# Expert jobs with a limit of 96 rows instead of 128 in a two-layer decoder kernel

## The reference

```python
def moe_swiglu(x, w_router, w_gate, w_up, w_down):
    B, S, D = x.shape                       # 1, 256, 1024
    xt = x.reshape(B * S, D)
    logits = jnp.matmul(xt, w_router, preferred_element_type=jnp.float32)
    top_vals, top_idx = lax.top_k(logits, TOP_K)          # 2 of 8
    top_w = jax.nn.softmax(top_vals, axis=-1)
    gates = jnp.sum(jax.nn.one_hot(top_idx, N_EXPERTS, dtype=jnp.float32) * top_w[..., None], axis=1)
    out = jnp.zeros((B * S, D), jnp.float32)
    for e in range(N_EXPERTS):
        y = swiglu(xt, w_gate[e], w_up[e], w_down[e]).astype(jnp.float32)   # D_FF = 3584
        out = out + gates[:, e:e + 1] * y
    return out.astype(x.dtype).reshape(B, S, D)
```

## Time and profile before

| | us |
|---|---|
| median of 3 runs | 1458.99 (1458.88 to 1460.97) |
| the profiled execution | 1458.9 |
| of it: up to the first expert matmul | 494.9 |
| one job, from its row transposes to those of the next | 119.3 |
| TensorE busy | 1442.7 |
| DVE, ACT, POOL busy | 1142.1, 970.2, 110.0 |

### The profile page before, as it was taken

One profiled execution on the slowest core, in us unless ns is written; L12 is line 12 of the kernel. 1 busy time (PEld: TensorE's weight loads), 2 busy tenths in 40 slices (PEclk: granted clock), 3 DMA queues, 4 the chain that ended last, 5 costly groups with the idle time before them and its releaser, 6 DMA issues.

```text
span 1458.9 us, 19214 instructions
## 1 busy us (share of the span) xinstructions
PE 1442.7 (99%) x6982; PEld 1189.6 (82%) x6982; DVE 1142.1 (78%) x841; ACT 970.2 (66%) x820; POOL 110.0 (8%) x186
## 2 busy tenths in 40 slices
PE   9999999999999999999999999999999999999998
PEld 7857888888998888888888888888888888888886
DVE  5756445545555798989898899989898999888997
ACT  5445444334566677777787787787777778777775
POOL 3002000001000540010010010010001001000001
PEclk9999999999999999999999999999999999999999
DMA  8709555553643599999999999999999999999995
GB/s 263 273 1 331 196 179 173 197 192 115 217 145 116 183 382 384 362 394 383 364 383 394 363 371 397 369 362 399 383 353 388 388 369 376 392 371 364 383 380 189
DMA packets 177458, 445.88 MB, mean 306 GB/s; under 512 B 8770, under 2 KB 19074, under 8 KB 161284
## 3 DMA queue, kind: packets, MB, share of 16 engines
q1 hardware_dynamic: 173440, 431.56, 81.4%
q0 software_dynamic: 3968, 13.69, 2.7%
q10 hardware_dynamic: 4, 0.01, 0.0%
HBM read 437.33 MB, written 7.90 MB: 305 GB/s over the span
## 4 chain that ended last, share of the span: by engine, by line
PE 91%; DVE 3%; ACT 3%; issue 2%; DMA 0%; ACTq 0%; POOL 0%; DVEq 0%
PE psum L485 27%; PE psum L487 27%; PE psum L486 27%; PE psum L608 2%; PE psum L1070 2%; ACT w_hi L1252 2%; DVE w_lo L1670 1%; PE psum L444 1%; PE psum L467 1%; PE psum L797 0%; PE psum L788 0%; PE psum L474 0%; PE psum L721 0%; PE psum L1102 0%; PE psum L855 0%
## 5 line engine op out<-in xcount | busy, mean ns | idle before, releaser
L1670 DVE TENSOR_TENSOR w_lo<-raw,w_hi 128x2048 fp32r<-128x2048 f32 x378 | 861.9, 2292 | 180.2 <-ACT w_hi L1252 179.0
L1252 ACT ACTIVATE w_hi<-raw 128x2048 fp32r<-128x2048 f32 x378 | 724.6, 1919 | 270.4 <-PE psum L487 270.3
L485 PE MATMUL psum<-w_hi,x_hi 128*128 128x512 f32 (+2 forms) x1216 | 476.7, 392 | 2.9 <-DVE w_lo L1670 2.6
L487 PE MATMUL psum<-w_hi,x_lo 128*128 128x512 f32 (+2 forms) x1216 | 470.0, 386 | 0.0
L486 PE MATMUL psum<-w_lo,x_hi 128*128 128x512 f32 (+2 forms) x1216 | 469.3, 386 | 0.0
L485 PEld LDWEIGHTS psum<-w_hi,x_hi 128*128 128x128 f32 x1216 | 228.4, 188 | 50.2 <-DVE w_lo L1670 5.5
L487 PEld LDWEIGHTS psum<-w_hi,x_lo 128*128 128x128 f32 x1216 | 228.3, 188 | 46.1
L486 PEld LDWEIGHTS psum<-w_lo,x_hi 128*128 128x128 f32 x1216 | 228.7, 188 | 43.0
L485 PE MATMUL psum<-w_hi,h_hi 128*128 128x512 f32 x576 | 225.3, 391 | 0.0
L487 PE MATMUL psum<-w_hi,h_lo 128*128 128x512 f32 x576 | 224.2, 389 | 0.0
L486 PE MATMUL psum<-w_lo,h_hi 128*128 128x512 f32 x576 | 224.1, 389 | 0.0
(11 more groups left out here) (276 smaller groups left out, 971.8 us busy)
## 6 DMA issues: line engine op xcount, KB each, us to landing
raw<-in_l_w_gate SPq DMA_DIRECT2D x126, 1024.0 KB, 7.3
raw<-in_l_w_up SPq DMA_DIRECT2D x126, 1024.0 KB, 7.6
raw<-in_l_w_down SPq DMA_DIRECT2D x126, 1024.0 KB, 7.2
raw<-in_l_w_in SPq DMA_DIRECT2D x10, 1024.0 KB, 6.4
raw<-in_l_w_out SPq DMA_DIRECT2D x8, 1024.0 KB, 5.9
raw<-in_l_w_in SPq DMA_DIRECT2D x6, 768.0 KB, 14.2
raw<-in_l_w_mem_kv SPq DMA_DIRECT2D x4, 1024.0 KB, 5.9
ys<-xn SPq DMA_DIRECT2D x4, 512.0 KB, 8.5
```

The costliest lines, as they stand in the source:

```text
L485: pe.matmul(out, x[0], w[0], start=first, stop=False, skip_group_check=True)
L487: return pe.matmul(out, x[1], w[0], start=False, stop=last, skip_group_check=True)
L1252: act.activation(w_hi[:, m % CUT, :], raw[:, n % RAW, :], ACT.Copy).then_inc(hi_ok, 1)
L1670: dve.tensor_tensor(w_lo[:, m % CUT, :], raw[:, n % RAW, :], w_hi[:, m % CUT, :].bitcast(F32), ALU.subtract).then_inc(lo_ok, 1)
```

## The change

`CAP` goes from 128 to 96. A job keeps at most 96 rows of an expert; rows 96 to 191 go to a second job and the rest to a third. Everything that is indexed by a job's rows gets 96: stationary columns, output partitions, the columns of the transposed blocks and of their splits (384 instead of 512), the rows of the indirect transfers. A job still owns 128 slots of the table, the last 32 unused. Five extra jobs are possible instead of three, so the tables have 14 blocks instead of 12, and DVE and POOL work out the extra jobs in another way. The weights, their pieces, the three passes and the 512 streaming columns are as they were.

```diff
-CAP = P
-MAX_JOBS = NE + NE // 2 - 1
+CAP = 96
+MAX_OVER = 2 * S // (CAP + 1)
+MAX_JOBS = NE + MAX_OVER
...
-                            ins = pe.matmul(bank(4 + hf, c * P, (c + 1) * P), rows[:, tt, k * P:(k + 1) * P],
-                                            pick[:, tt, :], start=(tt == 0), stop=(tt == NT - 1))
+                            ins = pe.matmul(bank(4 + hf, c * CAP, (c + 1) * CAP), rows[:, tt, k * P:(k + 1) * P],
+                                            pick[:, tt, 0:CAP], start=(tt == 0), stop=(tt == NT - 1))
...
-                            ins = thrice(bank(bb), (picked_hi[:, k, :], picked_lo[:, k, :]),
+                            ins = thrice(psum[0:CAP, bb, :], (picked_hi[:, k, :], picked_lo[:, k, :]),
                                          [y[:, c, :] for y in w], k == 0, k == KD - 1)
...
-                        ins = pe.transpose(bank(7, c * P, (c + 1) * P), hid1[:, b % 2, c * P:(c + 1) * P],
-                                           ident[:, :])
+                        ins = pe.transpose(bank(7, c * CAP, (c + 1) * CAP), hid1[0:CAP, b % 2, c * P:(c + 1) * P],
+                                           ident[0:CAP, 0:CAP])
...
-                            h = [y[:, b % 2, cc * P:(cc + 1) * P] for y in (h_hi, h_lo)]
-                            ins = thrice(bank(hf), h, [y[:, c, hf * 512:(hf + 1) * 512] for y in w],
+                            h = [y[:, b % 2, cc * CAP:(cc + 1) * CAP] for y in (h_hi, h_lo)]
+                            ins = thrice(psum[0:CAP, hf, :], h, [y[:, c, hf * 512:(hf + 1) * 512] for y in w],
                                          b == 0 and cc == 0, b == NB - 1 and cc == CB - 1)
...
-                            ins = pe.transpose(bank(4 + hf, c * P, (c + 1) * P), x_rows[:, k * P:(k + 1) * P],
-                                               ident[:, :])
+                            ins = pe.transpose(bank(4 + hf, c * CAP, (c + 1) * CAP),
+                                               x_rows[0:CAP, k * P:(k + 1) * P], ident[0:CAP, 0:CAP])
...
-                        act.activation(act1[:, b % 2, :], bank(bk.at["g", b][0]), ACT.Silu)\
+                        act.activation(act1[0:CAP, b % 2, :], psum[0:CAP, bk.at["g", b][0], :], ACT.Silu)\
...
-                            raise_part(("T", b - 1), h_hi[:, (b - 1) % 2, :], bank(7), j)
+                            raise_part(("T", b - 1), h_hi[:, (b - 1) % 2, 0:CB * CAP], bank(7, 0, CB * CAP), j)
...
-                link(pool.tensor_scalar(expert_at[:, :], iota_s[:, 0:NE], float(CAP), None, ALU.mult))
-                pool.tensor_scalar(moved_by[:, :], over[:, 2, :], float(CAP), float((NE - 2) * CAP), ALU.mult, ALU.add)
+                pool.tensor_scalar(expert_at[:, :], iota_s[:, 0:NE], float(P), None, ALU.mult)
+                link(pool.tensor_tensor(moved_by[:, :], over[:, 2, :], over[:, 3, :], ALU.subtract))
                 for tt in range(NT):
-                    ins = pool.tensor_scalar(second[:, tt, :], slot_of[:, tt, :], float(CAP), None, ALU.is_ge)
-                link(ins)
+                    pool.tensor_scalar(second[:, tt, :], slot_of[:, tt, :], float(CAP), None, ALU.is_ge)
+                    pool.tensor_scalar(third[:, tt, :], slot_of[:, tt, :], float(2 * CAP), float(P - CAP),
+                                       ALU.is_ge, ALU.mult)
+                link(pool.tensor_scalar(moved_by[:, :], moved_by[:, :], float(P), float(NE * P - CAP),
+                                        ALU.mult, ALU.add))
...
-                        out=x_rows, out_offset=None, in_=xs,
-                        in_offset=bass.IndirectOffsetOnAxis(ap=take_i[:, 0:1], axis=0)).then_inc(rows_in, 16)
+                        out=x_rows[0:CAP, :], out_offset=None, in_=xs,
+                        in_offset=bass.IndirectOffsetOnAxis(ap=take_i[0:CAP, 0:1], axis=0)).then_inc(rows_in, 16)
```

More of the change, by code:

```diff
@@ L179, in trunk @@
         rank = sb("rank", [P, NT, NE])
-        over = sb("over", [P, 3, NE])
-        over_sel = sb("over_sel", [P, 3, NE])
+        over = sb("over", [P, 4, NE])
+        over_sel = sb("over_sel", [P, MAX_OVER, NE])
         junk8 = sb("junk8", [P, 16])
@@ L189, in trunk @@
         last_f = sb("last_f", [P, 1])
-        job_f = sb("job_f", [P, 4])
-        job_i = sb("job_i", [P, 4], I32)
+        job_f = sb("job_f", [P, MAX_OVER + 1])
+        job_i = sb("job_i", [P, MAX_OVER + 1], I32)
         entry = sb("entry", [P, NT, 2, 4], I32)
@@ L1026, in _ @@
             pe.wait_ge(tables_ok, 1)
-            n_jobs = pe.value_load(job_i[0:1, 3:4], min_val=NE, max_val=MAX_JOBS)
+            n_jobs = pe.value_load(job_i[0:1, MAX_OVER:MAX_OVER + 1], min_val=NE, max_val=MAX_JOBS)
             def expert_job(j, last):
@@ L1496, in _ @@
             act.wait_ge(tables_ok, 1)
-            n_jobs = act.value_load(job_i[0:1, 3:4], min_val=NE, max_val=MAX_JOBS)
+            n_jobs = act.value_load(job_i[0:1, MAX_OVER:MAX_OVER + 1], min_val=NE, max_val=MAX_JOBS)
             def others_high(tt):
@@ L1531, in expert_job @@
                             act.wait_ge(gate_ok, 1)
-                            act.activation(y_parts[0][:, hf * 512:(hf + 1) * 512], bank(hf), ACT.Copy,
-                                           scale=gate_last[:, 0:1]).then_inc(y_hi_ok, 1)
+                            act.activation(y_parts[0][0:CAP, hf * 512:(hf + 1) * 512], psum[0:CAP, hf, :], ACT.Copy,
+                                           scale=gate_last[0:CAP, 0:1]).then_inc(y_hi_ok, 1)
                         others_high(1)
@@ L1538, in expert_job @@
                         full(("y", 0))
-                        act.activation(y_sb[:, 0:512], bank(0), ACT.Copy, scale=gate_of[:, bass.ds(j, 1)])\
+                        act.activation(y_sb[0:CAP, 0:512], psum[0:CAP, 0, :], ACT.Copy,
+                                       scale=gate_of[0:CAP, bass.ds(j, 1)])\
                             .then_inc(bk.empty_sem(("y", 0)), 1)
@@ L1949, in _ @@
             link(dve.tensor_scalar(over[:, 1, :], over[:, 0, :], float(CAP), None, ALU.is_gt))
-            link(dve.tensor_tensor_scan(over[:, 2, :], ones[:, 0:NE], over[:, 1, :], 0.0, ALU.mult, ALU.add))
-            for o in range(3):
-                ins = dve.scalar_tensor_tensor(out=over_sel[:, o, :], in0=over[:, 2, :], scalar=float(o + 1),
-                                               in1=over[:, 1, :], op0=ALU.is_equal, op1=ALU.mult)
-            link(ins)
-            for o in range(3):
-                link(dve.scalar_tensor_tensor(out=junk8[:, 0:NE], in0=iota_s[:, 0:NE], scalar=1.0,
-                                              in1=over_sel[:, o, :], op0=ALU.mult, op1=ALU.mult,
-                                              accum_out=job_f[:, o:o + 1]))
-            link(dve.tensor_scalar(job_f[:, 3:4], over[:, 2, NE - 1:NE], float(NE), None, ALU.add))
+            link(dve.scalar_tensor_tensor(out=over[:, 3, :], in0=over[:, 0, :], scalar=float(2 * CAP),
+                                          in1=over[:, 1, :], op0=ALU.is_gt, op1=ALU.add))
+            link(dve.tensor_tensor_scan(over[:, 2, :], ones[:, 0:NE], over[:, 3, :], 0.0, ALU.mult, ALU.add))
+            dve.tensor_scalar(job_f[:, MAX_OVER:MAX_OVER + 1], over[:, 2, NE - 1:NE], float(NE), None, ALU.add)
+            link(dve.tensor_tensor(over_sel[:, :, :], over[:, 2, :].unsqueeze(1).to_broadcast((P, MAX_OVER, NE)),
+                                   iota_s[:, 0:MAX_OVER].unsqueeze(2).to_broadcast((P, MAX_OVER, NE)), ALU.is_le))
+            link(dve.tensor_reduce(job_f[:, 0:MAX_OVER], over_sel[:, :, :], AX.X, ALU.add))
             dve.tensor_copy(job_i[:, :], job_f[:, :]).then_inc(tables_ok, 1)
@@ L1963, in gathered @@
                 part = (slice(None), slice(4 * hf, 4 * hf + 4), slice(None))
-                lower_part(label, picked_lo[part], bank(4 + hf).rearrange("p (k s) -> p k s", k=4),
+                lower_part(label, picked_lo[part], bank(4 + hf, 0, 4 * CAP).rearrange("p (k s) -> p k s", k=4),
                            picked_hi[part], j)
@@ L1984, in _ @@
             dve.wait_ge(tables_ok, 1)
-            n_jobs = dve.value_load(job_i[0:1, 3:4], min_val=NE, max_val=MAX_JOBS)
+            n_jobs = dve.value_load(job_i[0:1, MAX_OVER:MAX_OVER + 1], min_val=NE, max_val=MAX_JOBS)
             parts_before = n_part[0]
@@ L2126, in expert_rows @@
                 link(ins)
+                link(pool.tensor_tensor(second[:, :, :], second[:, :, :], third[:, :, :], ALU.add))
                 pool.tensor_tensor(slot_of[:, :, :], slot_of[:, :, :], second[:, :, :], ALU.add).then_inc(slots_ok, 1)
@@ L2151, in expert_rows @@
                 pool.wait_ge(tables_ok, 1)
-                n_jobs = pool.value_load(job_i[0:1, 3:4], min_val=NE, max_val=MAX_JOBS)
+                n_jobs = pool.value_load(job_i[0:1, MAX_OVER:MAX_OVER + 1], min_val=NE, max_val=MAX_JOBS)
                 pool.wait_ge(cleared, 16 * (SLOTS // P))
@@ L2168, in expert_rows @@
                     pool.indirect_dma_start(
```

(6 more changed lines are left out.)

37 lines of the change are left out of this document (20 added, 17 removed).

## The result

The changed kernel took 1464.39 us (median of 7 runs, 1463.08 to 1465.09), the kernel before beside it 1458.99 (7 runs, 1458.88 to 1463.19). The ratio is 1.0023, 95% interval 1.0014 to 1.0033: slower by some 3.4 us, where 1451.4 was predicted. The two medians stand further apart, by 5.4 us, because four of the seven runs before lie within 0.12 us of 1458.9 and the other three between 1460.2 and 1463.2; the ratio is not that of these two medians. Run once more on another chip it took 1464.23 against 1460.68 (ratio 1.0031, 1.0021 to 1.0040).

A forecast was written before the change was run, and what follows sets the result against it. TensorE's queue was taken to bound the kernel, in 8 expert jobs. From 1458.9 us, 7.5 for shorter transposes came off and all else counted 0, giving 1451.4 us; the range was 1449.0 to 1459.4.

The forecast's parts named there:

- The 504 matmuls: Expert matmuls of each job on TensorE: spacing stays 226.6 ns because the weight load is hidden; gain taken as 0.
- The transposes: 280 TensorE transposes streaming 96 identity columns instead of 128: 26.7 ns less each, 7.5 us gained in all.
- forecast job of 118.3 us: Length of one expert job after the change, down from 119.3 us through 36 transposes shorter by 0.0267 us each.
- What lies beside: Casts, `Silu`, product, copies and row gathers beside TensorE's queue: 0 gained, at most 0.1 us per job lost.
- the tables: Table work on DVE and POOL ahead of the first job: 0 to 0.5 us left for it.
- The wait for `w_lo`: TensorE's wait for DVE in each job: claimed to stay at 0.4 us.
- 1.1 us of cover for 0.8 us: Ahead of the first job: POOL's four added operations, about 0.2 us each, fit before DVE wants the result.
- (a): Rival: part of the expert matmuls' spacing is visible load and falls with stationary columns; another 13.4 us, 1438.0; 8%.
- (b): Rival: transposes don't get shorter, as the load or a fixed cost sets their 110 ns; 1458.9, no change; 9%.
- (c): Rival: TensorE drains between 96-column matmuls and 96-row transposes, 0.28 us for each of 56 blocks; 15.7 us more, 1467.1; 6%.
- (d): Rival: an expert exceeds 96 rows and a ninth job runs, 118.3 us more, 1569.7; with some unnamed slower surprise, 3%.
- The 9% given to slower: Chance given to the changed kernel being slower than the kernel before, made up of (c) and (d).

## Why the prediction was wrong

**1. The 504 matmuls: this step failed.** It took the spacing as unchanged and bounded the cost from 0 to a gain of 13.4 us. The loss side, which an operation not in the trace of before needs as well, was left without a bound. The change made them 2.6 ns (x) and 4.9 ns (h) longer, 1.70 us per job and about 14 us over the 4032 matmuls. The argument for 0 was that a hidden load of 188 ns becomes a hidden load of 161. That is true, and it answers another question: the experiments with 128 columns at 96 apart (232.5 ns) and 96 columns from column 31 (226.7) show that the spacing doesn't follow the load's length but the columns that it reads, together with what stood ahead of the stream. The trace of before held a hint that I didn't use: the same 228 to 236 ns in the first matmuls behind every block of transposes. A mean of 226.6 over 48 hides that this spacing is a settled state and that there are others.

Why certain columns cost time isn't shown. That the moving operand's reads and the load's reads of SBUF hinder each other would fit that a shift by 64 columns changes nothing and a shift by 32 does; no run here looks at that directly. The Trainium skill, in "TensorE: Matmul & The Clock Gate", section Step-by-step: what each phase is for, says that the two have separate read ports and that loading the next weights takes no SBUF read bandwidth from the running matmul. The bf16 streams agree as far as they go, 215.8 ns at both widths. In fp32r the load is felt: with the moving side untouched, its start column alone moved the spacing from 226.7 to 233.3. Whether that is read bandwidth, the runs can't tell.

**2. The transposes: right.** 82 ns instead of the forecast 82.9, and 0.56 us instead of 0.67 for each block of four; with the spacing kept by full loads, they bring 0.80 us per job, and 5.4 and 6.3 us in the medians. The forecast job of 118.3 us was met where the spacing was kept with loads of 96, in all jobs but the first from column 9.

**3 and 4. What lies beside, and the tables: right.** The wait for `w_lo` even halved, to 0.2 us, since TensorE got slower: it is 0.40 us in the version with loads of 128. Ahead of the first job DVE did wait, 0.29 us for POOL's `slot_of`, where 1.1 us of cover for 0.8 us had been counted (its own chain had become shorter too), and its slack paid: its next `w_lo` waits 0.95 us for ACT. From the first expert matmul back to the span's start the two traces differ by run to run, not by the change: 494.9 us before, 493.2 after, and 493.1 to 497.3 in the later kernels.

**The span and the median.** I let the profiled 1458.9 us stand for the median of 1458.99. Span and time aren't the same: the changed kernel's profiled span of 1460.9 belongs to a run of 1463.12, 2.2 us more. Of the kernel before, later runs with a span of 1458.9 took 1460.68 to 1460.75 us, so its profiled execution was a run near 1460.7. That is 1.8 us of error in any case, whatever the change does. In the experiments the kernel before has its medians at 1460.4 to 1460.9.

**The rivals.** None is what happened. (a), the load shows, and (b), transposes gain nothing, are wrong by their own rows. (c) was on the right side with the wrong mechanism: from the last transpose's start to the second matmul it is 0.31 us, the former 0.34 less the shorter transpose, so no drain is seen; what is lost is lost in the stream. (d) did not occur. The 9% given to slower stood on (c) and on (d) with its surprise that had no name; it was this one.

## What to carry to other kernels

In a stream of fp32r matmuls that change their weights each time, the place of the stationary blocks is worth as much as their width: load 128 columns from blocks that begin at column 0 and stand 128 apart (settled at 226.7 ns in every stream here; from column 1, 16 or 32 the same blocks gave 232.5 to 233.3), or measure the form that you want, in its own order, before you narrow it. A change that shortens what is hidden has also to be asked what it does to the rhythm of what is not. The version that takes the short transposes and keeps the full loads has 1454.3 to 1455.0 us, 0.35 to 0.39% under before. Loads of 96 from column 31 are as fast (1454.95), but parts of their jobs ran at 233.3 ns.

## What the hardware showed that was not expected

- Lasting spacings of 226.7, 228.9, 230.0, 231.7 and 233.3 ns, among others, for fp32r matmuls of 512 moving columns, chosen by the columns that the loads read and by what stood ahead; behind a wait of 0.39 us a stream went from 226.7 to 233.3.
- 96 stationary columns were slower than 128 at 512 moving columns (230.0 and 226.7), equal at 448 (202.7) and 320 (146.7), and faster at 416 (186.7 and 188.4) and 256 (116.0 and 120.0), one stream of each.
- Transposes of 96 rows queue at 82 ns, those of 128 at 109 ns, while single ones are recorded with 246 and 273.
- A kernel whose loads begin at column 9 had runs 13 us apart, all at granted clocks from 0.996 to 0.999.
